# Moving TensorE's token operands by 8 to 40 words, and streaming each weight product as alternating runs of 16 columns from its two halves

## What is computed

```
proj = einsum('btd,dn->btn', n, w_in)          # first block, 8280 columns
... gated delta rule, top-k attention ...
merged = sigmoid(gate_a) * (y_gdn @ w_branch_gdn) + sigmoid(gate_b) * (y_dsa @ w_branch_dsa)
h = h + rmsnorm(merged @ w_out)
u = square(relu(n2 @ w_up));  h = h + rmsnorm(u @ w_down)      # 4096 wide
# second block: layer 0 (short convolution, memory attention, dense swiglu 2816 wide),
# shared keys and values, layer 1 (block attention, memory attention), then
for e in range(8):                              # top-2 router
    out = out + gates[..., e:e + 1] * (silu(g) * u) @ w_down[e]   # g, u: x @ w_gu[e], 2816 wide
```

## Time and profile before

| | us |
|---|---|
| time before, median of 3 runs (lowest, highest) | 1777.97 (1777.48, 1783.62) |
| the profiled execution, its own time | 1777.92 |
| its span in the trace | 1776.1 |
| PE busy | 1754.1 (99%) |
| DVE busy | 1363.0 (77%) |
| ACT busy | 1076.1 (61%) |
| DMA, mean over the span | 252 GB/s |

### The profile page before, as it was taken

How to read it: one execution, slowest core, us unless ns; L and a number is a source line. 1 busy time by engine, 2 the same in 40 slices (tenths; PEclk the granted TensorE clock), 3 DMA queues, 4 the chain that set the end, 5 groups by cost and what they waited for, 6 DMA issues and landing times.

```text
span 1776.1 us, 26513 instructions
## 1 busy us (share of the span) xinstructions
PE 1754.1 (99%) x11249; PEld 1579.0 (89%) x11249; DVE 1363.0 (77%) x1591; ACT 1076.1 (61%) x1200; POOL 158.2 (9%) x165
## 2 busy tenths in 40 slices
PE   9999999999999999999999999999999999999997
PEld 8999999999988999998998888888888888888885
DVE  6895598577664667655687899888889898889897
ACT  7754455455544454444446777777777776767774
POOL 1454270000000100000030100000000000000110
PEclk9999999999999999999999999999999999999999
DMA  9342464656556555575463599999999999999994
GB/s 288 119 116 64 124 184 143 211 180 189 181 188 202 190 164 167 183 235 178 132 201 130 202 380 376 380 336 383 372 381 341 385 370 384 332 381 376 379 390 171
DMA packets 265206, 447.90 MB, mean 252 GB/s; under 512 B 11461, under 2 KB 135848, under 8 KB 264952
## 3 DMA queue, kind: packets, MB, share of 16 engines
q1 hardware_dynamic: 263464, 440.36, 71.1%
q0 software_dynamic: 1616, 5.77, 0.8%
HBM read 438.99 MB, written 4.73 MB: 250 GB/s over the span
## 4 chain that ended last, share of the span: by engine, by line
PE 91%; DVE 5%; ACT 2%; issue 1%; DMA 0%; SPq 0%; DVEq 0%; ACTq 0%
PE bank L428 27%; PE bank L430 27%; PE bank L429 27%; DVE ring_r L418 2%; PE bank L3240 1%; ACT hi_ring L403 1%; PE bank L2522 1%; PE bank L3154 1%; PE bank L1348 1%; PE bank L1340 1%; DVE arena L923 1%; PE bank L1832 1%; PE bank L2503 0%; PE bank L2152 0%; PE bank L1817 0%
## 5 line engine op out<-in xcount | busy, mean ns | idle before, releaser
L418 DVE TENSOR_TENSOR ring_r<-ring,hi_ring 128x2048 fp32r<-128x2048 f32 x401 | 905.4, 2284 | 264.7 <-ACT hi_ring L403 264.2
L403 ACT CAST hi_ring<-ring 128x2048 fp32r<-128x2048 f32 (+1 forms) x404 | 757.2, 1904 | 136.3 <-PE bank L430 129.3
L428 PE MATMUL bank<-hi_ring,arena_r 128*128 128x512 f32 (+1 forms) x1526 | 569.2, 373 | 2.0 <-DVE ring_r L418 2.0
L429 PE MATMUL bank<-ring_r,arena_r 128*128 128x512 f32 (+2 forms) x1534 | 567.5, 370 | 0.0
L430 PE MATMUL bank<-hi_ring,arena_r 128*128 128x512 f32 (+1 forms) x1526 | 566.7, 371 | 0.0
L428 PE MATMUL bank<-ring_r,hi_ring 128*128 128x256 f32 (+1 forms) x1400 | 398.9, 285 | 0.0
L430 PE MATMUL bank<-ring_r 128*128 128x256 f32 (+1 forms) x1400 | 395.2, 282 | 0.0
L429 PE MATMUL bank<-ring_r,hi_ring 128*128 128x256 f32 (+1 forms) x1400 | 395.0, 282 | 0.0
L428 PEld LDWEIGHTS bank<-hi_ring,arena_r 128*128 128x128 f32 x1526 | 286.8, 188 | 54.9 <-DVE ring_r L418 4.8
L429 PEld LDWEIGHTS bank<-ring_r,arena_r 128*128 128x128 f32 (+1 forms) x1534 | 287.9, 188 | 51.0
L430 PEld LDWEIGHTS bank<-hi_ring,arena_r 128*128 128x128 f32 x1526 | 286.9, 188 | 50.2
(11 more groups left out here) (436 smaller groups left out, 1572.7 us busy)
## 6 DMA issues: line engine op xcount, KB each, us to landing
ring<-in_w_gu_moe SPq DMA_DIRECT2D x176, 1024.0 KB, 7.3
ring<-in_w_down_moe SPq DMA_DIRECT2D x88, 1024.0 KB, 6.0
ring<-in_w_in SPq DMA_DIRECT2D x31, 1024.0 KB, 5.5
ring<-in_w_gu_dense SPq DMA_DIRECT2D x22, 1024.0 KB, 5.2
ring<-in_w_up SPq DMA_DIRECT2D x16, 1024.0 KB, 5.5
ring<-in_w_down SPq DMA_DIRECT2D x16, 1024.0 KB, 5.0
ring<-in_w_in_a SPq DMA_DIRECT2D x10, 1024.0 KB, 5.8
ring<-in_w_down_dense SPq DMA_DIRECT2D x10, 1024.0 KB, 5.0
```

What stands on the lines that cost most here:

```text
L403: q.e.copy(hi_ring[:, b:b + m], ring[:, a:a + m]).then_inc(*q.did(("hi", of.tag, i)))
L418: q.e.tensor_tensor(ring_r[:, a:a + m], ring[:, a:a + m], hi_ring[:, b:b + m].bitcast(F32), ALU.subtract).then_inc(*q.did(("lo", of.tag, i)))
L428: q.e.matmul(ps, a[0], b[0], start=first, stop=False)
L429: q.e.matmul(ps, a[0], b[1], start=False, stop=False)
```

## The change

`mm3` views its PSUM destination and both parts of its moving operand in another order, if their width is a multiple of 128: as two halves, and in each 16 columns at a time, so that the stream runs over columns 0 to 15 of the first half, 0 to 15 of the second, 16 to 31 of the first, and so on. The destination is permuted in the same way, so each result lands where it did. Products 272 columns wide stay as they were. The stationary operands are read as before.

`X` becomes an area of its own shape at word 16 behind the ring's slots, 8 rows of 256 words without gaps. With that, all its rows and, by the new offsets, `yg`, `yd`, `mg`, `u_`, `mix2`, `gg` and `memT` start at 24 modulo 32, where `xs2` and `hp` were. (`nX` stays, so its rows are at 8 and 24 in turn.) The other new offsets make room.

No instruction is added, removed or moved on any engine, and no wait is. Two splits that wrote rows of `X` as 2 x 256 words now write 512 in one run.

```
-    X = Pair(nX.hi[:, :, 0:SEQ], nX.lo[:, :, 0:SEQ])
+    X = Pair(*[shaped(ring_r[:, o:o + 8 * SEQ], (8, SEQ)) for o in (NRAW * BLK + 16, NRAW * BLK + 16 + 8 * SEQ)])
...
+    def paired_lines(a):
+        return a.rearrange("p (h j e) -> p j h e", h=2, e=16) if a.shape[1] % P == 0 else a
+
     def mm3(q, ps, a, b, first, last):
-        q.e.matmul(ps, a[0], b[0], start=first, stop=False)
-        q.e.matmul(ps, a[0], b[1], start=False, stop=False)
-        return q.e.matmul(ps, a[1], b[0], start=False, stop=last)
+        ps, high, low = [paired_lines(v) for v in (ps, b[0], b[1])]
+        q.e.matmul(ps, a[0], high, start=first, stop=False)
+        q.e.matmul(ps, a[0], low, start=False, stop=False)
+        return q.e.matmul(ps, a[1], high, start=False, stop=last)
...
-    yg = pair_at(2176, 8, SEQ)
+    yg = pair_at(2168, 8, SEQ)
...
-    yd = pair_at(8576, 8, SEQ)
+    yd = pair_at(8568, 8, SEQ)
...
-    mg, xin2 = pair_at(13056, 8, SEQ), at(17152, 2, 1024)
+    mg, xin2 = pair_at(13016, 8, SEQ), at(17152, 2, 1024)
...
-    u_, dn = pair_at(2048, 32, SEQ), at(18432, 2, 1024)
+    u_, dn = pair_at(2072, 32, SEQ), at(18456, 2, 1024)
...
-    mix2 = pair_at(6656, 8, SEQ)
+    mix2 = pair_at(6616, 8, SEQ)
...
-    memT, memin = pair_at(22376, 8, SEQ), at(2176, 2, 1024)
+    memT, memin = pair_at(22328, 8, SEQ), at(2176, 2, 1024)
...
-    gg = pair_at(6656, 22, SEQ)
+    gg = pair_at(6616, 22, SEQ)
```

More of the change, by code:

```diff
@@ L532, in emit @@
     wT, vn, ktm = AT, D, AT[:, 0:8, :]
-    yg = pair_at(2176, 8, SEQ)
+    yg = pair_at(2168, 8, SEQ)
     rhT, hn = at(6272, P)[0:16, :], [at(o, 512) for o in (13056, 13568, 14080, 16768)]
     sq2 = [flat(AT[:, 2 * j:2 * j + 2, :]) for j in range(8)]
-    aq = at(6528, 8, SEQ)
-    yd = pair_at(8576, 8, SEQ)
+    aq = at(6520, 8, SEQ)
+    yd = pair_at(8568, 8, SEQ)
     iq, ik, ak, av = at(19456, 4, SEQ), at(22528, T), at(22800, 2, T), at(14896, 3, 256)
@@ L551, in emit @@
     mix_sq, x2_sq, r_mix, r_x2 = at(12672, 2, 4), at(12680, 2, 2), at(12684, 2), at(12686, 2)
-    u_, dn = pair_at(2048, 32, SEQ), at(18432, 2, 1024)
-    ut = [at(18432 + SEQ * j, SEQ) for j in range(4)]
-    dn_gain, dn_junk, dn_sq, r_dn = at(21248, 1024), at(20992, 256), at(22272, 2, 4), at(22280, 2)
+    u_, dn = pair_at(2072, 32, SEQ), at(18456, 2, 1024)
+    ut = [at(18456 + SEQ * j, SEQ) for j in range(4)]
+    dn_gain, dn_junk, dn_sq, r_dn = at(21272, 1024), at(21016, 256), at(22296, 2, 4), at(22304, 2)
     xr, xv = at(0, 2, 1024), at(2048, 2, 1024)
@@ L571, in emit @@
     mv_raw = [at(18944, 4, SEQ), at(21304, 4, SEQ)]
-    mv_later = [Pair(at(6656 + 1024 * h, 4, SEQ, of=arena_r), at(o, 4, SEQ, of=arena_r)) for h, o in ((0, 18944), (1, 21304))]
-    ang, kf = at(20480, SEQ), at(20736, SEQ)
+    mv_later = [Pair(at(6616 + 1024 * h, 4, SEQ, of=arena_r), at(o, 4, SEQ, of=arena_r)) for h, o in ((0, 18944), (1, 21304))]
+    ang, kf = at(20504, SEQ), at(20760, SEQ)
     qm = at(13856, 2, SEQ)
@@ L583, in emit @@
     lg, m8b, gt2, oh = at(8192, 2, 8), at(8208, 2, 8), at(8224, 2, 8), at(8240, 2, 2, 8)
-    ixf, sel, ge, posm, cnt = at(8272, 2, 8), at(8288, 2, 8), at(8304, 2, 8), at(8320, 2, 8), at(8336, 8)
+    ixf, sel, ge, posm, cnt = at(8272, 2, 8), at(9176, 2, 8), at(9192, 2, 8), at(9208, 2, 8), at(9224, 8)
     lgT = at(8344, SEQ)
```

## The result

The changed kernel takes 1822.94 us, median of 4 runs (1820.87 to 1824.35), against 1779.08 us for the kernel before on the same chip. The ratio is 1.0244, with a 95% interval of 1.0231 to 1.0258. I had forecast 1718 us. The time went the other way, and past the upper end of the range.

What follows compares the result with a forecast made beforehand. PE's matmuls were taken to bound the kernel; 32 us (256 columns), 7 us (512 columns before the experts) and 21 us (experts) sum to 60 us off 1777.97, giving 1718 us, range 1693 to 1778.

Steps and rivals of the forecast that it cites:

- What bounds the kernel: Whole kernel: PE, busy 1754.1 of 1776.1 us, is the bound; in the experts DMA stands close behind.
- The excess per matmul: In mm3, each matmul takes 11 to 21 ns beyond its columns' streaming time, and operand addresses affect the time.
- A candidate for the excess: In mm3, the next stationary operand's load starts 0.01 us after the running matmul, so two streams read the same memory.
- that clash: Load and moving stream collide in the same 16 of 32 words; plain streams half the time, paired streams at 24 never.
- The term of 256 columns: Before the experts, 4692 products fall by 0.0072 us each towards 0.111 us: 32 us less after chain losses.
- The term of 512 columns before the experts: 702 products fall by 0.0123 us each to 0.222 us: 8.6 us, cut to 7 us by DMA.
- the experts: Eight experts' products get shorter, PE alone saving 24 us; 21 us taken because DMA interruptions may reach PE.
- The limit by DMA: Weight loads reach at most 390 GB/s, 2.69 us per 1024 KB; PE would want a block every 2.66 us.
- the second rival: Only the new offsets act, 3.7 us on 702 products and 1 us on token streams: 1773 us, chance 0.14.
- breaks cost: The paired stream's jumps, in reading and in PSUM, cost one or two columns each: 1795 or 1875 us, chance 0.18.
- No clash: The excess depends on where operands start, not on column order; only offsets act: 1773 us, chance 0.14.
- The range: Whole kernel's time: 1693 to 1778 us, meant to leave out 2 in 10.

## Why the prediction was wrong, point by point

**What bounds the kernel: right.** PE was the bound before and after, every change of the time was the products' price times their count, and DMA and DVE followed.

**The excess per matmul: seen rightly, explained wrongly.** That a matmul takes 11 to 21 ns more than its columns, and that the operands' addresses reach the time, stood in the rows. The step that failed is the next: "A candidate for the excess is in the earlier trace rows". I had two rows that showed a load and a stream side by side, none that showed that the load took anything from the stream, and I made all three terms of the sum from it. With a load of a quarter of the length, the excess stays: 231.1 ns for 229.0, and 240.0 for 240.0 paired. The step also went against the rows it stood on: by that clash a plain stream loses half of the time wherever it starts, and then and the earlier trace rows could not have differed. The rule of the Trainium skill, "TensorE: Matmul & The Clock Gate", section "Step-by-step: what each phase is for", that a load takes no read bandwidth from the running matmul, agrees with these rows of 512 columns. The residues of the two operands do matter together (229.0 to 234.1 ns), which the rule does not tell.

**The term of 256 columns**, 32 us less: it went to 120.0 ns, not 111, and is 9 us more. **The term of 512 columns before the experts**, 7 us less, is 4 us more; **the experts**, 21 us less, are 33 us more. I took 0.222 us for a clash-free 512; the paired stream costs 0.240.

**The limit by DMA** was worked out for nothing, since PE never asked for more. It stays untested. Before the experts it was also worked out wrongly: there two groups of 128 tokens use each block, so 1024 KB last for 24 matmuls and not 12, which at 0.222 us is 197 GB/s and nowhere near 390. The trace before shows it in the MLP's down projection, last number:

```profile
495.00:535.00 40.00, 40.00 (x172) 32.17 (x171) 25.41 (x29) 14.50 (x12) 0.00 (x0) 1.00 0.51 173
```

The term should have been 8.6 us, not 7.

**The offsets** were priced at 5 us less in the second rival; alone they give 8.4 us less, with the reservation above.

**The rival "breaks cost"** was right in sign, and its two times, 1795 and 1875, lie on both sides of 1823. I gave it 0.18. Its mechanism as I wrote it fell: PSUM isn't charged, and the price is not by the jump. A price by the column of a broken fp32r stream was on no list. "No clash", with the paired stream as cheap as the plain one, fell as well.

**The range** did not reach to the slower cases, though I had no row with a paired stream. Where an edit touches 8754 products and its unit price is in no row, 1 ns is 9 us; the bounds should have been those of that price on both sides.

**What stays open.** Why a reordered fp32r read costs 18 slots of 0.42 ns for 16 columns instead of 16, why a hole of 2 words costs 257.8 and one of 4 words 240.0, what the plain stream's excess of 11 to 21 ns is made of, and what makes one plain pattern cost 113.3 or 117.8 ns. Every stretch had a load before each matmul, if a short one; none had no load at all. The prices are measured, the mechanism isn't.

## What to carry to other kernels

Leave a moving fp32r operand in one unbroken run of addresses: reordered in runs of 16 it cost 5% of a 512-column matmul, whatever the offsets, and runs of 16 with holes between them cost 3 to 13%. Then try the residue of the two operands modulo 32 words in the kernel itself; 16 words apart was the cheapest in this one, and where the experts' tokens lie, in steps of 4 to 24 words, was worth up to 15 us of 1780 without touching an instruction. Measure a new access pattern's price alone before building a sum on it: a program of 24 matmuls for each pattern foretold the paired 512 columns of the kernels within 0.1 ns, though not the plain ones.

## What the runs showed of the hardware that I had not expected

- An fp32r stream and a bf16 stream have different prices at the same clock: 229 and 215.8 ns for 512 columns, 118 and 109.2 for 256.
- fp32r reads in runs of 16 columns from two halves cost 7.5 ns a run, at every start and, within 0.1 ns a run, at every width from 128 to 512; in bf16 they cost no more than a plain stream.
- Writing PSUM in runs of 16 is free for 512 columns: 229.3 ns for 228.9.
- Some mean prices of plain streams are whole multiples of 6.67 ns (113.3, 120.0, 226.7, 233.3), and others lie between (116.7, 117.8, 228.9, 231.1).
